# Expert sums: from three slots of eight on VectorE to every second slot

## The reference, cut to what matters

```python
# x: 1072 tokens, processed in blocks; 8 heads, 16 experts each = 128 experts per token
v1, i1 = lax.top_k(s1, 16); v2, i2 = lax.top_k(s2, 16)      # per head, 128 keys each
sc, ci = lax.top_k(cand, 16)                                 # 256 candidate pairs
eidx = e1 * 128 + e2;  g = softmax(sc)
act = gelu(einsum('thkd,td->thk', expert_u[eidx], xt))       # dot of the token with each u row
w = g * act
out = einsum('thk,thkd->td', w, expert_v[eidx])              # weighted sum of the v rows
```

## Time and profile before

| | before |
|---|---|
| median of 3 runs | 4677.8 us |
| profiled execution | 4673.28 us, span 4671.5 us |
| PE busy | 3487.8 us (75%) |
| VectorE (DVE) busy | 2752.9 us (59%) |
| ScalarE (ACT) busy | 1220.1 us (26%) |
| mean granted TensorE clock | 0.816 |
| memory traffic | 1331.91 MB, 285 GB/s over the span |

### The profile page before, as it was taken

The page is one execution under the profiler, slowest core; times in us unless marked ns, Lnnn a source line. Parts: engine busy times, 40 slices in busy tenths (PEclk is TensorE's granted clock), DMA queues, the critical chain, the costliest instruction groups (busy, mean ns, idle before and its releaser), DMA issues.

```text
span 4671.5 us, 32805 instructions
## 1 busy us (share of the span) xinstructions
PE 3487.8 (75%) x10062; PEld 1792.2 (38%) x10062; DVE 2752.9 (59%) x5414; ACT 1220.1 (26%) x2631; POOL 1447.0 (31%) x1213
## 2 busy tenths in 40 slices
PE   6799997758983788888478888865887678745564
PEld 4344443524461444445134444532444334412221
DVE  2200001367479677658976775699665655996665
ACT  1111102135211445311145552111444431110100
POOL 0111000024222344333433332344222234444553
PEclk9999997767896787798767778987676789877877
DMA  3122111469876899899888989998787789989997
GB/s 122 55 72 93 72 54 39 167 249 349 324 301 231 317 368 379 356 369 380 312 329 326 358 307 375 392 346 331 274 311 273 262 339 385 389 317 357 420 420 288
DMA packets 251084, 1331.91 MB, mean 285 GB/s; under 512 B 29880, under 2 KB 73144, under 8 KB 104448
## 3 DMA queue, kind: packets, MB, share of 16 engines
q0 software_dynamic: 163232, 1142.47, 62.5%
q1 hardware_dynamic: 87680, 187.35, 11.3%
HBM read 1294.07 MB, written 35.10 MB: 285 GB/s over the span
## 4 chain that ended last, share of the span: by engine, by line
PE 28%; DVE 27%; DMA 13%; ACT 6%; issue 6%; SPq 2%; POOL 1%; DVEq 0%; ACTq 0%; POOLq 0%
PE pv L869 12%; DVE uv L1249 11%; DMA uv<-expert_uv,rows_u 7%; PE pb L978 4%; PE pb L851 4%; PE pb L951 3%; DVE held L1273 3%; PE pb L822 2%; PE pb L926 2%; DMA arena<-w_stream 2%; DVE arena L1240 2%; SPq L700 2%; DMA arena<-out_sv_p 1%; POOL uv L776 1%; DMA uv<-expert_uv,rows_pk 1%
## 5 line engine op out<-in xcount | busy, mean ns | idle before, releaser
L776 POOL DMA_INDIRECT uv<-expert_uv,rows_u x1024 | 1311.2, 1280 | 2461.7 <-PE pv L869 1511.8
L869 PE MATMUL pv<-uv,diag 128*128 128x512 f32 x2640 | 1566.4, 753 | 598.7 <-ACT diag L1093 528.6
L1249 DVE CUSTOM_DVE_ANT_0 uv<-uv,nr 128x1024 f32<-128x1024 f32 x1056 | 1241.8, 1220 | 277.1 <-DMA uv<-expert_uv,rows_u 237.8
L869 PEld LDWEIGHTS pv<-uv,diag 128*128 128x128 f32 x2640 | 624.1, 246 | 1431.3 <-issue 1348.8
L248 PE MATMUL ps<-win,xg 128*128 128x512 f32 (+1 forms) x1440 | 631.8, 597 | 0.0
L1100 ACT ACTIVATE gel<-dots 128x4 f32<-128x4 f32 x264 | 54.2, 205 | 2049.4 <-DVE dots L1249 2049.2
L1273 DVE SCALAR_TENSOR_TENSOR held<-uv,wgt,held 128x1024 f32<-128x1024 f32 x387 | 497.3, 1285 | 13.6 <-DVE wgt L1260 0.3
L822 PE MATMUL pb<-arena 64*128 64x512 f32 (+6 forms) x544 | 265.3, 590 | 294.8 <-DMA arena<-out_sv_p 111.9
L248 PEld LDWEIGHTS ps<-win,xg 128*128 128x128 f32 (+1 forms) x1440 | 261.1, 184 | 343.9 <-issue 343.6
L851 PE MATMUL pb<-arena 128*128 128x64 f32 (+3 forms) x1728 | 320.5, 349 | 34.3 <-ACT o L1082 33.7
L851 PEld LDWEIGHTS pb<-arena 128*128 128x128 f32 (+3 forms) x1728 | 287.7, 245 | 52.9 <-issue 39.3
(11 more groups left out here) (163 smaller groups left out, 2562.8 us busy)
## 6 DMA issues: line engine op xcount, KB each, us to landing
arena<-w_stream SPq DMA_DIRECT2D x80, 1024.0 KB, 9.0
win<-w_main SPq DMA_DIRECT2D x10, 2048.0 KB, 8.8
uv<-expert_uv,rows_u POOLq DMA_INDIRECT x1024
scratch_gates<-stage POOLq DMA_DIRECT2D x32, 256.0 KB, 2.3
arena<-scratch_gates SPq DMA_DIRECT2D x8, 1024.0 KB, 22.4
xg<-x_t SPq DMA_DIRECT2D x8, 536.0 KB, 7.6
arena<-scratch_c_p SPq DMA_DIRECT2D x8, 520.0 KB, 8.0
xr<-x SPq DMA_DIRECT2D x8, 512.0 KB, 3.8
```

Of the source, the lines that this page charges most:

```text
L776: pool.indirect_dma_start(out=uv[k % NU][:].rearrange("p a n -> p (a n)"), out_offset=None, in_=io["expert_uv"][:, :], in_offset=bass.Indi ...
L869: mm = nc.tensor.matmul(pv[:, c * BANK:(c + 1) * BANK], diag[n % ND][:], uv[k % NU][:, 1, c * BANK:(c + 1) * BANK], start=n == first, stop ...
L1249: nc.vector.tensor_tensor_reduce(out=u, in0=u, in1=row[:], scale=1.0, scalar=0.0, op0=ALU.mult, op1=ALU.add, accum_out=dots[b % 2][:, k % ...
```

## The change

VectorE takes slots 0 and 2 of every lot, PE slots 1 and 3. Every lot, even or odd, then has two and two. 132 slots, one in each even lot, move from PE (and their diagonals from ScalarE) to VectorE: 528 on each. In odd lots the count stays, but slot 2 takes the place of slot 1 on VectorE.

```diff
     def on_dve(self, k):
         j = k % NK
-        return j % LOT == 0 or (j % LOT == 1 and j // LOT % 2 == 1)
+        return j % 2 == 0
```

## The result

| | median us | lowest to highest | runs | profiled execution | span | mean granted clock |
|---|---|---|---|---|---|---|
| before | 4677.8 | 4673.9 to 4682.86 | 5 | 4673.28 | 4671.5 | 0.816 |
| after | 4711.19 | 4698.84 to 4716.36 | 5 | 4712.22 | 4710.4 | 0.793 |

The change makes the kernel 0.67% slower: ratio 1.0067, 95% interval 1.005 to 1.0083, or 23 to 39 us. The forecast was 4684 us with a range of 4656 to 4708, so the time lies 3 us above the range. It falls near the value of rival C (4713), and part of C's mechanism is in it, but at other places than C had it.

What follows compares the result with a forecast made beforehand. No engine bounds the whole: VectorE sets experts steps, a loop attention, memory the last stretch. Experts steps +31.7 us, less relief in attention, merges and last stretch, plus +3 for gather order, gave +6 us: median 4684 us, range 4656 to 4708.

Steps and rivals of the forecast that it cites:

- rival C: Gather queue in tiles 3 to 8: odd lots' late third gather costs 1 us in each of 21 periods; 4713 us, chance 0.13.
- Experts steps: Halves and experts steps: VectorE alone sets the time, one more sum in about 24 even lots; +31.7 us.
- First attention halves: Even lots' smaller PE blocks on the chain: tiles 5 and 6 -6.3 us, tiles 1 and 2 -9, tiles 3 and 4 0.
- Second half of tiles 5 and 6: Attention there: the even lot lies in the other step, off the chain, so nothing is gained.
- the clock: PE's granted clock in attention: taking work from PE was given no cost, from 0.75 with larger blocks against 0.79 with smaller.
- Tiles 7 and 8: Attention there: period's parts as in tiles 5 and 6, partly covered by key and value loads; -4 us, bounds 0 and -6.3.
- Order of the gathers: GpSimd's queue: an odd lot's gather goes 8 us later, mostly hidden by some 10 us of slack; +3 us, bounds 0 and +21.
- Merges and queries: Merge steps gain from shorter even PE blocks, -7 us; query steps 0, as the memory share is 1.01, bound -15.
- rival A: PE's relief counts everywhere, query steps included, and tiles 3, 4, 7 and 8 gain as well; -22 us, 4656 us, chance 0.27.
- Last stretch: End of the kernel: memory alone limits and VectorE has time to spare; -2 us, bounds -5 and 0.
- B: Attention of tiles 3 to 8 gives nothing back, as waits for keys and expert rows take over; +17 us, 4695 us, chance 0.22.
- GpSimd beside VectorE: New VectorE sums stretch up to 132 gathers by 0.92 us, 121 us of GpSimd time; adds nothing to the sum.

Runs made afterwards that it cites:

- e3: The changed kernel, but halves and experts steps keep three of eight slots on VectorE as before the change; ratio 1.0039 to before, 4691.3 us.
- e5: VectorE has slots 0 and 1 of every lot, but three of eight slots in halves and experts steps; 4653.5 us, ratio 0.9962 to before.
- e1: The changed kernel's amount in another order: VectorE sums slots 0 and 1 of every lot; 4681.59 us, ratio 1.0024 to before.
- e4: The changed kernel plus zero-matrix products on PE in even lots of the second attention halves of tiles 3 to 8; 4704.89 us, ratio 1.0071 to before.
- e9: No VectorE sums in halves and experts steps (a tile's first slot aside), slots 0 and 1 elsewhere; 4618.98 us, ratio 0.9894 to before.
- e10: As e9, but the kernel before's three of eight in lots 112 to 129 and 194 to 209; 4609.26 us, ratio 0.9871 to before.
- e2: The kernel before with its amounts kept, but VectorE has slots 0 and 2 in odd lots instead of 0 and 1; 4696.3 us, ratio 1.0057.
- e6: The kernel before, but VectorE sums only slot 0 of each lot in halves and experts steps; 4670.77 us, ratio 0.9989.
- e7: The kernel before, but VectorE sums nothing in halves and experts steps except a tile's first slot; 4627.89 us, ratio 0.9913.

## Why the prediction was wrong, point by point

*Experts steps: right.* +31.7 us by 24 x 1.32 of the earlier trace rows, +33.0 measured, and three of eight instead of four takes 28 of it away again (e3, e5). The search steps hold 25 even lots (4 and three times 7), and 25 x 1.32 is 33.0. The search of tiles 3 and 4 is 9.3 us longer, for the 8 that were foretold from six even lots; it has seven. L1273 in 2180 to 2352 us after the change, for the 24.51 (x20) of the earlier trace rows:

```profile
2180.00:2352.00 172.00, 32.21 (x26) 0.69 0.80 307
```

*First attention halves: right in mechanism.* In tiles 5 and 6 -6.3 was summed from the earlier trace rows and -9.0 came; in tiles 1 and 2 -9 against -4.7 (e1, in the better order, -8.5); in tiles 3 and 4 0 against -5.1. The periods in tiles 5 and 6 are 28.0 us, not the 27.5 that the direct comparison of the two halves promised.

*Second half of tiles 5 and 6: wrong.* The prediction had "nothing is gained there" and left it at 0, since the even lot is off the chain. It lost 14.3 us. The failed step is the clock, a term put at nothing: "the two stretches speak against a cost, and the sum has none". The earlier trace rows set 0.75 in one half against 0.79 in the other; but what was to be compared was the second half with itself, before and after, and that is 0.79 against 0.73. The two halves hold other work beside the blocks, so the comparison between them said nothing of taking blocks away. The page of the Trainium skill that I had set against my reading, "TensorE: Matmul & The Clock Gate", section "What's actually happening", has the clock follow PE's activity, and here the trace agrees with it: PE was busy 196.16 us in 235 before and 183.84 in 242 after, and was granted less clock. The zero products of e4 brought 0.77 and 7 us back, the step from e9 to e10 0.76 and 2 us. The rest of the 14.3 us is open; kernels that left this stage as it was also stand at +3.1 to +6.4 in it.

*Tiles 7 and 8: wrong in sign.* -4 was taken, +12.4 came in attention. With the slots in order 0, 1 it is -10.7 in e1 and -3.2 in e5, so the estimate of PE's relief was about right or too small, and what overrode it is the next step.

*Order of the gathers: the mis-sized term.* The prediction took +3 us with bounds 0 and +21, spread over 21 periods at up to 1 us. The runs put it at +20 (after against e1), +27 (e2 against before) and +36 (e5 against e3), at its upper bound or above it. By the profiles it lies not in 21 periods but for the most part in the attention of tiles 7 and 8, around the stalls of PE. The step that failed is the slack: "some 10 us" was set against a slip of 8 us. Gather 686 slipped by 22 us (33.9 for 12.1), and lot 171 came 13 us late in e2 (21.8 for 9.1) and 14 in after (24.1 for e1's 10.4). Where PE waits 15 us and more for keys, a queue whose head is a PE slot waits with it, and the slack is gone. Rows 9, which the step was read from, lie in the attention of tiles 5 and 6, where PE's longest wait is 8.1 us. The question to ask was what this queue does in the stage where PE stands longest. The sign that the prediction gave for this, a longer wait of VectorE's dots for gathers in attention, was hardly there against the kernel before: 64.8 us for 61.6 in the stretch of tiles 7 and 8, and over the whole span 225.9 for 237.8. It shows only against a kernel with the same amount of work, as e1 (168.8).

*Merges and queries: small as foretold*, -9.3 in the first three for the -7 of all, with the query steps held by memory at 413 GB/s: rival A is out. The last merge lost 7.9, which was not foreseen. It lost 3.8 to 7.9 in all kernels with two sums a lot there, but also +3.0, +3.1 and +6.6 in e2, e6 and e7, which have the rule of before there; so the cause is open.

*Last stretch: right.* The chain's gathers come every 19.96 us, as in the earlier trace rows, and the 40 lots take the same time:

```profile
4442.87 12.22 DMA uv<-expert_uv,rows_u
...
4462.83 12.21 DMA uv<-expert_uv,rows_u
```

*The rivals.* B (attention gives nothing, +17) is wrong: attention gives, and then loses by other means. C was given 0.13. Its mechanism, the third gather of an odd lot that goes out late, is what gather 686 shows, but few places pay for it and not every period; and had the order been priced at its upper bound with the rest of the sum as it stood, the forecast would have been 4702. The search steps' +33, the order's +20 and the relief of about -20 elsewhere (e1, +0.24% in all, less the search steps) make the +0.67%; the clock's loss is inside that -20. The nearness of C's 4713 to the measured 4711 is luck: C had no gain in the periods and 1 us of loss in each, where the runs show gains and a few large losses.

*GpSimd beside VectorE.* Gathers take 1326 ns in the mean, POOL is busy 1491.6 us for 1447.0: 45 us of the up to 121 that the prediction worked out. The new sums are not alone in this. In the kernel before, gathers issued while VectorE stood idle took 0.94 us in the mean (258 of them), those that overlapped mostly with L1273 1.44 us (152), and those that overlapped mostly with a dot, L1249, 1.52 us (362). No run shows that this alone costs time: e2 has nothing added on VectorE and the loss is there, e1 has all of it and the order's loss is not.

## What to carry to other kernels

When work is dealt out between two engines that free the same ring of buffers, the order of the slots is a parameter of its own beside the amount: let the engine that finishes on time hold the slots at the head of the queue, and try the order by itself, since here it was worth 20 to 36 us, and the amount alone, in the better order, 11. Price a queue's slack in the stage where the engine ahead of it stalls longest, not in the one where it is easiest to read. And deal out by stage: where one engine sets the pace alone (search steps), give it nothing; where a loop through several engines does, compare the stage with itself and not with its neighbour.

## What the runs showed of the hardware that was not expected

- With less background work TensorE was granted less clock for its foreground work: with blocks of eight instead of twelve in every second lot the clock of the stretch fell from 0.79 to 0.73, a score product took 647 ns for 603 in the mean, and the periods 28.4 us for 27.5. Products with zeros went with 0.77 and 27.5 us.
- Where memory alone sets the pace, the clock cost nothing: it fell from 0.80 to 0.69 in the last stretch, and the 40 lots took the same time.
- At one amount of work on each engine and one mean clock (0.787 to 0.794), the order of the buffers in GpSimd's queue moved the time by 1.8%: 1.0024, 1.0067 and 1.0201.
- Savings of 28 and of 75 us in the search steps went with a first attention half of tiles 5 and 6 that is 11 us longer in both, with no instruction changed there. It stays open why; e9 shows it too (+11.7), and e10, the same program up to there, only in part (+4.1).
